# Row-half products issued in pairs, and each attention head's output product moved ahead of a later head's scores

## The chip, the cores and the metric

One core of a Trainium2 chip runs the whole kernel. The metric is device time in microseconds of one execution; the median of the runs shown is compared. Engines are named as in the profile: PE (TensorE, with PEld for its weight loads), DVE (VectorE), ACT (ScalarE), POOL (GpSimd) and SP (SyncE, which issues the weight DMAs).

## What is computed

One encoder layer for 512 prompt tokens and 32 sample tokens (544 columns in all), in float32:

```
h = RMSNorm(x);  c = h @ w_in            # columns: RWKV-7 | q, k, v | gates A, B
A = RWKV-7 time mixing(c)                # per head matrix state, chunks of 64
s = q_n . k_n * 64**-0.5, n = 0, 1       # differential attention, 4 heads, 2 maps
o = (softmax(s_0) - lam * softmax(s_1)) @ v     # block-causal for the prompt
mix = sig(gA) * (A @ w_out_a) + sig(gB) * (RMSNorm(o) @ w_out_b)
x = x + RMSNorm(mix @ w_o);  x = x + RMSNorm(SwiGLU(RMSNorm(x)))
```

Outputs are the new x, the keys, the values and the RWKV states.

## The kernel before

Every large product ("dense") is made of float32 split in two parts, w_hi/w_lo and h_hi/h_lo, with three matmuls for each. POOL splits the weights, 128 columns at a time. The dense products of the whole layer are one long list, and all small work stands between them. The order is written out by hand: `schedule()` makes one list of steps, `SCHEDULE`, and each of the engines runs through the same list and issues its own part of every step. So the list sets the order on PE, and on ACT and DVE too. An engine issues its instructions in that order and waits at each for its semaphores.

Small products write to four PSUM banks, `side0` to `side3`, in a ring: the n-th fill (`FILL`, from `fills()`) uses bank n % 4, `open_bank` makes PE wait until the fill four before it was drained, `full_bank` makes the reader wait until the product is there, `drain` frees the bank and `landed` waits for a drain.

Attention has 16 prompt heads, numbered here 0 to 15: tiles t = 0 to 3 of 128 queries with 4 heads each, with 128(t+1) keys, then 4 heads of the sample tile. One head i consists of these steps:

- `attS` (S): PE makes the two score maps, m = 0 on partitions 0 to 63 and m = 1 on 64 to 127, one bank each (L1124). DVE sets the mask (L1703), takes the maximum (L1705) and scales it (L1706) for each map; ACT makes the exponentials with their sums (L1317), again one map after the other.
- `attC` (C): DVE combines both maps into the weights (L1717 to L1721), in one of two buffers `probs`.
- `attP` (P): PE transposes the weights (L1081, `side<-ident,early`, t+1 of them), ACT copies them to `pT` (L1327).
- `attO` (O): PE multiplies `pT` by v (L1150); it waits until the copy has drained its bank. ACT copies the result to `otok` (L1337) and takes its squares with their sum (L1338).

Between the steps stand pieces of the gate products gB and gA: `piece()` takes as many as `turns` says, 24 for these 16 heads. A piece, D below, is a quarter of a block of 128 columns, 12 matmuls of 272 columns; at the end of a block ACT makes a tanh of it (L1586) and issues its store. The loop for head i puts S two heads ahead:

```python
rows = [piece() + [("attP", *th)], piece()]
...attC(i + 1), attS(i + 2) at the end of the second row
rows += [piece() + [("attO", *th)] + ...]
```

Products that contract over 64 rows ("row halves": their operands stand on partitions 0 to 63 or on 64 to 127) are besides S: `rwA` (L1174: decay, f = "w", rows 0 to 63; and learning rate, f = "a", rows 64 to 127; two column halves each), four times; and in the RWKV part, for each tile t and each half g of the heads, `sk` (L911, f = "k", 256 columns) and `sb1` (L911, f = "r", 128 columns), with p for the row half. ACT's copies of step `tok` (L1421 to L1424) drain the four banks that `sk` then takes, and DVE drains `sk` (L1817) and `sb1` (L1809). An fp32 product stands in the profile as two MATMULs.

Of the kernel before, what the change touches and what calls it, by code (L numbers as in the profile page):

```python
# [9 lines left out]
ACT = mybir.ActivationFunctionType  # L10
# [9 lines left out]
HALF = TOK // 2  # L20
J = TOK + 1
# [11 lines left out]
BH, BD_, BV = 4, 64, 128  # L33
# [11 lines left out]
SAMPLE = NT - 1  # L45
# [156 lines left out]
def schedule():  # L202
# [7 lines left out]
    def spread(n, places):  # L210

        return [(i + 1) * n // places - i * n // places for i in range(places)]
# [31 lines left out]

    pieces = [dense(k, i, p, 4) for k in ("gB", "gA") for i in range(8) for p in range(4)]
    heads = [(t, h) for t in range(NT) for h in range(BH)]
    turns = [1] + spread(24, 3 * BH * SAMPLE) + [2, 1, 1, 1, 1, 0, 1, 1, 1, 1, 1, 1]

    def piece():
        n = turns.pop(0)  # L250
        out, pieces[:n] = pieces[:n], []
        return out
# [3 lines left out]
    for i, th in enumerate(heads):  # L256
        rows = [piece() + [("attP", *th)], piece()]
        if i + 1 < len(heads):
            rows[-1] += [("attC", *heads[i + 1])]
        if i + 2 < len(heads):  # L260
            rows[-1] += [("attS", *heads[i + 2])]
        rows += [piece() + [("attO", *th)] + ([("vtok", th[0] + 1)] if th[0] < SAMPLE and th[1] == 1 else [])]
        if th[0] < SAMPLE:
            s += sum(rows, [])
        else:
            sample += rows
# [55 lines left out]
def fills(step):  # L322

    k = step[0]
    if k == "params":
        return ["pv"]
    if k in ("normB", "zC"):
        return ["n0", "n1"]
    if k == "cache":
        return ["ck"]  # L330
    if k in ("ktok", "vtok"):
        return [k[0]]
    if k == "attS":
        return ["s0", "s1"]
    if k == "attP":
        return ["pt"]
    if k in ("ofin", "attO"):
        return ["o"]
    if k == "shiftout":
        return ["s"]  # L340
    if k == "knorm":
        return ["q0", "q1"]
    if k == "rwA":
        return ["w0", "w1", "a0", "a1"]
    if k == "rw2":
        return ["b0", "b1"]
    if k == "init":
        return ["s"]
    if k == "w":
        return {"tok": ["t0", "t1"], "sb0": ["b0", "b1"], "sb1": ["r0", "r1"], "sk": ["k0", "k1"], "xi": [], "ya": [],  # L350
                "gv": ["gv"], "wu": ["wu"], "e": ["e0", "e1"] if step[2] < SAMPLE else ["e0"], "chain0": ["c"],
                "chain1": ["c"], "q": ["q"], "yb": ["y"]}[step[1]]
    if k in ("wm", "wd", "wt"):
        return [k[1]]
    if k == "final":
        return ["f"]
    if k in ("ymean", "yvar"):
        return ["m"]
    if k == "yfin":
        return ["g"]  # L360
    if k == "ztok":
        return ["z0", "z1"]
    if k == "zw":
        return ["z"]
    return []
# [32 lines left out]
def encoder_kernel(nc, i_, o_):  # L398
# [40 lines left out]
    dtmp = sb("dtmp", [P, J], at=phase2)  # L439
# [24 lines left out]
    vtok = sb("vtok", [P, NT, BW], at=region)  # L464
# [28 lines left out]
    ossq = sb("ossq", [P, NT * BH], at=phase2)  # L493
# [8 lines left out]
    otok = sb("otok", [P, NT, BW], at=inner)  # L502
# [54 lines left out]
    def open_bank(pe, step, f):  # L557

        n = FILL[(step, f)]
        if n >= 4:  # L560
            pe.wait_ge(drained[n % 4], n // 4)
        return side[n % 4]
# [10 lines left out]
    def landed(eng, step, f):  # L573

        n = FILL[(step, f)]
        eng.wait_ge(drained[n % 4], n // 4 + 1)
# [267 lines left out]
    def wkv_pe(pe, step, transposes, close):  # L844

        t, g = step[2], step[3]
        n, j0 = TILES[t][1], first(t)
# [56 lines left out]
        elif st in ("sb1", "sk"):  # L904
            f, blk, us = ("r", CR, slice(1, 2)) if st == "sb1" else ("k", CK, slice(0, 2))
            m = n * (us.stop - us.start)
            for p in range(2):
                b = open_bank(pe, step, f"{f}{p}")
                lo, hi = 64 * p, 64 * p + 64
                for c in range(2):  # L910
                    ins = pe.matmul(b[0:n, c * m:(c + 1) * m].rearrange("p (u i) -> p u i", i=n),  # L911
                                    C[lo:hi, blk + 2 * g + c, 1 + j0:1 + j0 + n], AR[lo:hi, 2 * g + c, us, j0:j0 + n],
                                    start=True, stop=True)
                close(ins, step, f"{f}{p}")
        elif st == "gv":
            b = open_bank(pe, step, "gv")
            landed(pe, ("w", "tok", t, g), "t1")
# [75 lines left out]
    def _(pe):  # L993
# [91 lines left out]
        for step in SCHEDULE:  # L1085
# [81 lines left out]
            elif k == "rwA":  # L1167
                c = step[1]
                if c == 0:
                    pe.wait_ge(s_["lora_a"], 1)  # L1170
                for f, lo in (("w", 0), ("a", 64)):
                    for i, (a, b_) in enumerate(((0, HALF), (HALF, J))):
                        b = open_bank(pe, step, f"{f}{i}")
                        close(pe.matmul(b[:, 0:b_ - a], wa2[lo:lo + 64, c * P:(c + 1) * P],  # L1174
                                        C[lo:lo + 64, CWA, 1 + a:1 + b_], start=True, stop=True), step, f"{f}{i}")
# [65 lines left out]
    def _(act):  # L1241
# [11 lines left out]
        def drain(ins, step, f):  # L1253

            ins.then_inc(drain_sem(step, f), 1)
# [10 lines left out]
        for step in SCHEDULE:  # L1266
# [65 lines left out]
            elif k == "attO":  # L1332
# [1 line left out]
                _, t, h = step  # L1334
                n, idx = TILES[t][1], t * BH + h
                b = full_bank(act, step, "o")
                A(f_act(otok[0:n, t, h * BV:(h + 1) * BV], b[0:n, 0:BV], ACT.Copy))  # L1337
                drain(f_act(b[0:n, 0:BV], b[0:n, 0:BV], ACT.Square, accum_out=ossq[0:n, idx:idx + 1]), step, "o")  # L1338
            elif k == "oscale":
                n, a, b_ = ((P, 0, SAMPLE * BH), (DEC, SAMPLE * BH, NT * BH))[step[1]]  # L1340
                landed(act, ("attO", SAMPLE if step[1] else SAMPLE - 1, BH - 1), "o")
# [729 lines left out]
```

## Time and profile before

| | |
|---|---|
| median of 3 runs | 1038.54 us (1035.91 to 1040.54) |
| the profiled execution | 1040.89 us, its span 1039.1 us |
| PE busy | 993.6 us, 96% of the span |
| DVE, ACT, POOL busy | 451.2, 284.0, 557.1 us |
| granted clock of PE, mean | 0.996 |
| POOL waiting for PE | 366.2 us |

Busy time of PE counts overlapping matmuls once. A row of the timeline merges instructions of a kind that overlap: its start, the length from the first start to the last end, and behind the names the shapes and the count. "idle before" stands in square brackets.

### The profile page before, as it was taken

How to read it: one execution, taken by the hardware profiler on the slowest of the kernel's cores; microseconds unless marked ns; L12 is line 12 of the kernel's file. 1: busy time of each engine (PE TensorE's matmuls, PEld its weight loads, DVE VectorE, ACT ScalarE, POOL GpSimd, SP SyncE). 2: the span in 40 equal slices, each digit the busy share in tenths (PEclk: the TensorE clock that was granted, in tenths of full speed). 3: DMA queues.
4: the chain of work that ended last, by engine and by line, in shares of the span. 5: the costliest groups of instructions: out<-in, count | busy, mean ns of one | idle time of the engine just before them, and what ended most of it. 6: DMA issues, size and time to landing. Idle time of an engine off the chain costs nothing.

```text
span 1039.1 us, 22129 instructions
## 1 busy us (share of the span) xinstructions
PE 993.6 (96%) x8886; PEld 939.6 (90%) x8886; DVE 451.2 (43%) x878; ACT 284.0 (27%) x810; POOL 557.1 (54%) x608
## 2 busy tenths in 40 slices
PE   5999999999999999999989998999999999999997
PEld 5999999987878888888878898999999999999996
DVE  5466478277643555655355354333333333200003
ACT  5223444255554132332211353001101000011101
POOL 6667899633445224143257713655655655656571
PEclk9999999999999999999999999999999999999999
DMA  7332332432223101050115611223223223232332
GB/s 245 86 86 79 82 82 65 133 103 73 66 76 87 33 33 33 33 204 22 47 47 160 177 34 62 81 83 99 81 81 101 81 81 101 74 95 74 94 92 87
DMA packets 138111, 89.63 MB, mean 86 GB/s; under 512 B 5386, under 2 KB 130032, under 8 KB 138032
## 3 DMA queue, kind: packets, MB, share of 16 engines
q1 hardware_dynamic: 129508, 73.11, 24.6%
q10 hardware_dynamic: 8524, 15.42, 4.3%
q8 instruction: 56, 0.92, 0.4%
q14 instruction: 23, 0.19, 0.1%
HBM read 79.32 MB, written 9.19 MB: 85 GB/s over the span
## 4 chain that ended last, share of the span: by engine, by line
PE 82%; DVE 6%; POOL 4%; DMA 3%; ACT 3%; issue 1%; ACTq 0%; DVEq 0%; SPq 0%; POOLq 0%
PE dense L1005 66%; PE side L1081 3%; DMA w_raw<-in_w_o 2%; POOL w_lo L738 1%; PE side L1124 1%; PE side L1150 1%; PE side L957 1%; POOL S L738 1%; PE side L931 1%; PE side L921 1%; PE side L1201 1%; DMA xs<-in_x_prompt 1%; PE side L911 1%; PE side L871 1%; PE side L987 1%
## 5 line engine op out<-in xcount | busy, mean ns | idle before, releaser
L733 POOL TENSOR_SCALAR w_hi<-w_raw 128x256 fp32r<-128x256 f32 (+1 forms) x256 | 160.3, 646 | 374.7 <-PE dense L1005 366.2
L738 POOL TENSOR_TENSOR w_lo<-w_raw,w_hi 128x256 fp32r<-128x256 f32 (+1 forms) x256 | 320.8, 1276 | 9.8
L1005 PE MATMUL dense<-h_hi,w_hi 128*128 128x272 f32 (+2 forms) x1392 | 302.7, 295 | 4.4 <-DVE h_lo L1640 2.5
L1005 PE MATMUL dense<-h_hi,w_lo 128*128 128x272 f32 (+2 forms) x1392 | 293.8, 289 | 0.0
L1005 PE MATMUL dense<-h_lo,w_hi 128*128 128x272 f32 (+2 forms) x1392 | 293.1, 288 | 0.0
L1005 PEld LDWEIGHTS dense<-h_hi,w_hi 128*128 128x128 f32 x1392 | 220.9, 189 | 15.0 <-issue 7.0
L1005 PEld LDWEIGHTS dense<-h_lo,w_hi 128*128 128x128 f32 x1392 | 221.4, 189 | 0.0
L1005 PEld LDWEIGHTS dense<-h_hi,w_lo 128*128 128x128 f32 x1392 | 220.2, 189 | 0.0
L1005 PE MATMUL dense<-S,w_hi 128*128 128x272 f32 (+2 forms) x648 | 109.2, 289 | 0.1
L1005 PEld LDWEIGHTS dense<-S,w_hi 128*128 128x128 f32 x648 | 92.2, 188 | 0.5 <-issue 0.4
L1005 PE MATMUL dense<-S,w_lo 128*128 128x272 f32 (+2 forms) x324 | 68.2, 288 | 0.0
L2001 DVE SCALAR_TENSOR_TENSOR S<-z,S 128x544 f32 (+1 forms) x22 | 53.7, 2440 | 22.4 <-ACT S L1539 22.4
L1995 DVE TENSOR_TENSOR z<-z,dense 128x544 f32<-128x544 f32 (+2 forms) x23 | 15.9, 696 | 97.1 <-PE dense L1005 97.1
L1936 DVE TENSOR_TENSOR z<-side,gain 128x512 f32<-128x512 f32 x7 | 4.8, 692 | 114.6 <-ACT h_hi L1502 114.6
L1005 PEld LDWEIGHTS dense<-S,w_lo 128*128 128x128 f32 x324 | 51.1, 188 | 0.0
L1539 ACT ACTIVATE S<-z 128x544 f32 (+1 forms) x22 | 14.5, 659 | 132.3 <-DVE z L1995 132.3
L1005 PE MATMUL dense<-S 128*128 128x288 f32 (+1 forms) x336 | 45.3, 291 | 1.7 <-POOL S L738 1.7
L1005 PEld LDWEIGHTS dense<-S 128*128 128x128 f32 x336 | 42.8, 188 | 2.5 <-issue 2.2
L1990 DVE SCALAR_TENSOR_TENSOR z<-z,dense 128x544 f32<-128x544 f32 (+2 forms) x23 | 15.9, 697 | 59.0 <-ACT z L1532 55.1
L1532 ACT ACTIVATE z<-dense 128x544 f32<-128x544 f32 x21 | 13.1, 626 | 97.5 <-PE dense L1005 97.5
L816 POOL TENSOR_TENSOR AR<-AR 128x256 f32<-128x256 f32 (+1 forms) x10 | 6.5, 650 | 46.1 <-DVE AR L1889 46.1
L1317 ACT ACTIVATE early<-side,amax 128x128 f32<-128x128 f32 (+4 forms) x40 | 20.0, 499 | 34.8 <-DVE amax L1706 31.8
(269 smaller groups left out, 1392.6 us busy)
## 6 DMA issues: line engine op xcount, KB each, us to landing
w_raw<-in_w_ffn_in SPq DMA_DIRECT2D x44, 512.0 KB, 3.8
w_raw<-in_w_in SPq DMA_DIRECT2D x43, 512.0 KB, 3.9
w_raw<-in_w_ffn_out SPq DMA_DIRECT2D x16, 448.0 KB, 3.7
gates<-gst ACTq DMA_DIRECT2D x16, 272.0 KB, 2.1
w_raw<-in_w_o SPq DMA_DIRECT2D x8, 512.0 KB, 4.3
w_raw<-in_w_ffn_out SPq DMA_DIRECT2D x8, 512.0 KB, 3.8
w_raw<-in_w_out_a SPq DMA_DIRECT2D x5, 512.0 KB, 3.4
mb<-gates ACTq DMA_DIRECT2D x1, 2176.0 KB, 9.9
```

The lines of the kernel that those rows point to most:

```text
L733: ins = nc.gpsimd.tensor_scalar(hi[:, q], w_raw[:, slot, q], 1.0, 0.0, ALU.mult, ALU.add)
L738: ins = nc.gpsimd.tensor_tensor(lo[:, q], w_raw[:, slot, q], hi[:, q].bitcast(F32), ALU.subtract)
L871: ins = pe.matmul(b[32 * q:32 * q + 32, 0:64], xt[:, g, q, :], mce[:, g, q, :], start=True, stop=True)
L911: ins = pe.matmul(b[0:n, c * m:(c + 1) * m].rearrange("p (u i) -> p u i", i=n), C[lo:hi, blk + 2 * g + c, 1 + j0:1 + j0 + n], AR[lo:hi, 2 ...
L1005: ins = pe.matmul(acc[:, bk, 0:tn], w, r[:, t0:t0 + tn], start=first and n == 0, stop=final and n == 2)
L1081: ins = pe.transpose(b[0:m, c0:c0 + n], src, ident[0:n, 0:n])
L1317: drain(f_act(probs[0:n, pb, m, 0:keys], b[0:n, 0:keys], ACT.Exp, bias=amax[0:n, 2 * pb + m:2 * pb + m + 1], scale=SCALE, accum_out=asum[0 ...
L1532: f_act(f_t.rearrange("p (a b) -> p a b", a=2), pa[:, :, 0:HALF], ACT.Tanh, scale=0.5).then_inc(s_["f_tanh"], 1)
L1539: f_act(dst, f_s.unsqueeze(1), ACT.Copy, scale=0.5).then_inc(s_["f_hi"], 1)
L1990: ins = vec.scalar_tensor_tensor(out=fs, in0=ft, scalar=1.0, in1=ga_, op0=ALU.add, op1=ALU.mult)
L1995: ins = vec.tensor_tensor(fs, fs, gb_, ALU.mult)
L2001: vec.scalar_tensor_tensor(out=lo, in0=f_s.unsqueeze(1), scalar=0.5, in1=hi.bitcast(F32), op0=ALU.mult, op1=ALU.subtract).then_inc(s_["f_l ...
```

## The change

1. The order within a head. P(i), C(i+1), then O(i), and S(i+2) last. Before: P(i), C(i+1), S(i+2), O(i). `turns` now gives a head 0, 1 and i % 2 pieces: none ahead of P, one between P and O, and for an odd i one between O and S. Before it alternated 0, 1 over the three places, so that a pair of heads had 0, 1, 0 and 1, 0, 1. The sum is 24 in both. For the sample heads the same loop gives four rows a head in place of three, and these are woven with the steps of the RWKV inverse.
2. `rwA` and `sb1`/`sk` issue their products in turns of low and high row half, having opened both banks; the order of `FILL` for `rwA` follows.
3. In `attO`, ACT drains the bank with the copy, and takes the squares from `otok` in SBUF, into `dtmp`, no longer from the bank.

```diff
--- before.py
+++ after.py
@@ -244,7 +244,7 @@
 
     pieces = [dense(k, i, p, 4) for k in ("gB", "gA") for i in range(8) for p in range(4)]
     heads = [(t, h) for t in range(NT) for h in range(BH)]
-    turns = [1] + spread(24, 3 * BH * SAMPLE) + [2, 1, 1, 1, 1, 0, 1, 1, 1, 1, 1, 1]
+    turns = [1] + [n for i in range(BH * SAMPLE) for n in (0, 1, i % 2)] + [2, 1, 1, 1, 1, 0, 1, 1, 1, 1, 1, 1]
 
     def piece():
         n = turns.pop(0)
@@ -257,9 +257,8 @@
         rows = [piece() + [("attP", *th)], piece()]
         if i + 1 < len(heads):
             rows[-1] += [("attC", *heads[i + 1])]
-        if i + 2 < len(heads):
-            rows[-1] += [("attS", *heads[i + 2])]
-        rows += [piece() + [("attO", *th)] + ([("vtok", th[0] + 1)] if th[0] < SAMPLE and th[1] == 1 else [])]
+        rows += [[("attO", *th)] + ([("vtok", th[0] + 1)] if th[0] < SAMPLE and th[1] == 1 else [])]
+        rows += [piece() + ([("attS", *heads[i + 2])] if i + 2 < len(heads) else [])]
         if th[0] < SAMPLE:
             s += sum(rows, [])
         else:
@@ -341,7 +340,7 @@
     if k == "knorm":
         return ["q0", "q1"]
     if k == "rwA":
-        return ["w0", "w1", "a0", "a1"]
+        return ["w0", "a0", "w1", "a1"]
     if k == "rw2":
         return ["b0", "b1"]
     if k == "init":
@@ -904,14 +903,15 @@
         elif st in ("sb1", "sk"):
             f, blk, us = ("r", CR, slice(1, 2)) if st == "sb1" else ("k", CK, slice(0, 2))
             m = n * (us.stop - us.start)
-            for p in range(2):
-                b = open_bank(pe, step, f"{f}{p}")
-                lo, hi = 64 * p, 64 * p + 64
-                for c in range(2):
-                    ins = pe.matmul(b[0:n, c * m:(c + 1) * m].rearrange("p (u i) -> p u i", i=n),
+            b = [open_bank(pe, step, f"{f}{p}") for p in range(2)]
+            for c in range(2):
+                for p in range(2):
+                    lo, hi = 64 * p, 64 * p + 64
+                    ins = pe.matmul(b[p][0:n, c * m:(c + 1) * m].rearrange("p (u i) -> p u i", i=n),
                                     C[lo:hi, blk + 2 * g + c, 1 + j0:1 + j0 + n], AR[lo:hi, 2 * g + c, us, j0:j0 + n],
                                     start=True, stop=True)
-                close(ins, step, f"{f}{p}")
+                    if c == 1:
+                        close(ins, step, f"{f}{p}")
         elif st == "gv":
             b = open_bank(pe, step, "gv")
             landed(pe, ("w", "tok", t, g), "t1")
@@ -1168,8 +1168,8 @@
                 c = step[1]
                 if c == 0:
                     pe.wait_ge(s_["lora_a"], 1)
-                for f, lo in (("w", 0), ("a", 64)):
-                    for i, (a, b_) in enumerate(((0, HALF), (HALF, J))):
+                for i, (a, b_) in enumerate(((0, HALF), (HALF, J))):
+                    for f, lo in (("w", 0), ("a", 64)):
                         b = open_bank(pe, step, f"{f}{i}")
                         close(pe.matmul(b[:, 0:b_ - a], wa2[lo:lo + 64, c * P:(c + 1) * P],
                                         C[lo:lo + 64, CWA, 1 + a:1 + b_], start=True, stop=True), step, f"{f}{i}")
@@ -1334,8 +1334,9 @@
                 _, t, h = step
                 n, idx = TILES[t][1], t * BH + h
                 b = full_bank(act, step, "o")
-                A(f_act(otok[0:n, t, h * BV:(h + 1) * BV], b[0:n, 0:BV], ACT.Copy))
-                drain(f_act(b[0:n, 0:BV], b[0:n, 0:BV], ACT.Square, accum_out=ossq[0:n, idx:idx + 1]), step, "o")
+                drain(f_act(otok[0:n, t, h * BV:(h + 1) * BV], b[0:n, 0:BV], ACT.Copy), step, "o")
+                landed(act, step, "o")
+                A(f_act(dtmp[0:n, 0:BV], otok[0:n, t, h * BV:(h + 1) * BV], ACT.Square, accum_out=ossq[0:n, idx:idx + 1]))
             elif k == "oscale":
                 n, a, b_ = ((P, 0, SAMPLE * BH), (DEC, SAMPLE * BH, NT * BH))[step[1]]
                 landed(act, ("attO", SAMPLE if step[1] else SAMPLE - 1, BH - 1), "o")
```

PE in tile 3, around the scores of head 14 (`qkv 128x512`; `vtok,pT` is an O, `ident,early` a P). Before:

```order
L1124 MATMUL side<-qkv 128x512 x2
L1150 MATMUL side<-vtok,pT 128x128 x4
L1005 MATMUL dense<-h_hi,w_hi 128x272 x2
L1005 MATMUL dense<-h_lo,w_hi 128x272 x2
L1005 MATMUL dense<-h_hi,w_lo 128x272 x2
L1005 MATMUL dense<-h_hi,w_hi 128x272 x2
L1005 MATMUL dense<-h_lo,w_hi 128x272 x2
L1005 MATMUL dense<-h_hi,w_lo 128x272 x2
L1081 MATMUL side<-ident,early 128x128 x4
L1124 MATMUL side<-qkv 128x512 x2
```

After:

```order
L1150 MATMUL side<-vtok,pT 128x128 x4
L1124 MATMUL side<-qkv 128x512 x2
L1081 MATMUL side<-ident,early 128x128 x4
L1005 MATMUL dense<-h_hi,w_hi 128x272 x2
L1005 MATMUL dense<-h_lo,w_hi 128x272 x2
L1005 MATMUL dense<-h_hi,w_lo 128x272 x2
L1005 MATMUL dense<-h_hi,w_hi 128x272 x2
L1005 MATMUL dense<-h_lo,w_hi 128x272 x2
L1005 MATMUL dense<-h_hi,w_lo 128x272 x2
L1150 MATMUL side<-vtok,pT 128x128 x4
```

Before, the rows are S(14), O(12), a piece, P(13), S(15), and O(13) comes only after one more piece. After, they are O(12), S(14), P(13), a piece, O(13).

ACT over the same heads (`early,asum` are the two exponentials of a head, `pT` the copy of a P, `otok` that of an O). Before:

```order
L1327 ACTIVATE pT<-side 128x512
L1586 ACTIVATE gst<-dense,pvh 128x544
L1589 DMA gates<-gst 128x544
L1317 ACTIVATE early,asum<-side,amax 128x512 x2
L1337 ACTIVATE otok<-side 128x128
L1338 ACTIVATE side,ossq<-side 128x128
L1327 ACTIVATE pT<-side 128x512
L1317 ACTIVATE early,asum<-side,amax 128x512 x2
```

After:

```order
L1327 ACTIVATE pT<-side 128x512
L1587 ACTIVATE gst<-dense,pvh 128x544
L1590 DMA gates<-gst 128x544
L1337 ACTIVATE otok<-side 128x128
L1339 ACTIVATE dtmp,ossq<-otok 128x128
L1317 ACTIVATE early,asum<-side,amax 128x512 x2
L1327 ACTIVATE pT<-side 128x512
L1337 ACTIVATE otok<-side 128x128
```

Before, the rows begin with `pT` of head 12 and the tanh; the exponentials are those of head 14, then `otok` of 12, `pT` of 13 and the exponentials of 15. After, they begin with the same two, and `otok` of 12 has moved ahead of the exponentials of 14, with `pT` and `otok` of 13 behind them. In both orders `pT` of head i+1 stands behind the exponentials of head i+2.

## Rows read from the trace of the kernel before

**Rows 1.** The page, parts 1 and 2: TensorE's busy time and granted clock.

```profile
PE 993.6 (96%) x8886; PEld 939.6 (90%) x8886; DVE 451.2 (43%) x878; ACT 284.0 (27%) x810; POOL 557.1 (54%) x608
...
PEclk9999999999999999999999999999999999999999
```

**Rows 2.** Timeline, tile 3: start us, length us, engine, line, operation, tiles, count.

```profile
257.08 0.60 PE L1081 MATMUL side<-ident,early 128*128 128x128 f32 x4
...
259.04 0.59 ACT L1327 ACTIVATE pT<-side 128x512 f32<-128x512 f32 x1
...
259.11 1.13 PE L1124 MATMUL side<-qkv 64*128 64x512 f32 x4
...
260.17 1.16 PE L1150 MATMUL side<-vtok,pT 128*128 128x128 f32 x8
...
260.46 0.11 DVE L1703 MEMSET side<- 64x64 f32 x1
...
261.08 0.49 PE L1005 MATMUL dense<-h_hi,w_hi 128*128 128x272 f32 x2
...
262.67 0.60 PE L1081 MATMUL side<-ident,early 128*128 128x128 f32 x4
262.69 0.69 ACT L1317 ACTIVATE early<-side,amax 128x512 f32<-128x512 f32 x1 [0.33 <-DVE amax L1706]
...
263.20 1.45 PE L1124 MATMUL side<-qkv 64*128 64x512 f32 x4
...
264.85 0.75 DVE L1721 SCALAR_TENSOR_TENSOR early<-early,arec 128x512 f32<-128x512 f32 x1
```

**Rows 3.** Timeline, tile 0, second head.

```profile
202.27 0.49 PE L1124 MATMUL side<-qkv 64*128 64x128 f32 x4
...
202.69 0.52 PE L1005 MATMUL dense<-h_hi,w_hi 128*128 128x272 f32 x2
202.91 0.11 DVE L1703 MEMSET side<- 64x64 f32 x1 [1.48 <-PE side L1124]
...
204.33 0.37 ACT L1317 ACTIVATE early<-side,amax 128x128 f32<-128x128 f32 x1 [0.24 <-DVE amax L1706]
```

**Rows 4.** Timeline, tile 2: a copy of weights and the output products behind it.

```profile
239.69 0.48 ACT L1327 ACTIVATE pT<-side 128x384 f32<-128x384 f32 x1
...
240.28 0.91 PE L1150 MATMUL side<-vtok,pT 128*128 128x128 f32 x6
```

**Rows 5.** ScalarE by form, 202 to 269.5 us: xcount | busy us, mean ns.

```profile
L1327 ACT ACTIVATE pT<-side 128x128 f32<-128x128 f32 x4 | 1.1, 273 | 1.4 <-DVE vtok L1690 1.4
```

**Rows 6.** TensorE by form, the same stretch: score products.

```profile
L1124 PE MATMUL side<-qkv 64*128 64x512 f32 x16 | 5.8, 641 | 0.0
L1124 PE MATMUL side<-qkv 64*128 64x384 f32 x16 | 5.0, 535 | 0.0
L1124 PE MATMUL side<-qkv 64*128 64x256 f32 x16 | 4.0, 428 | 0.0
...
L1124 PE MATMUL side<-qkv 64*128 64x128 f32 x12 | 2.0, 323 | 0.0
```

**Rows 7.** Timeline of TensorE: a full-row fp32 product, then the other row-half products.

```profile
57.56 1.08 PE L1165 MATMUL side<-AR,cst 128*128 128x272 f32 x4
...
116.67 1.20 PE L1174 MATMUL side<-C,wa 64*128 64x272 f32 x8
...
327.26 3.00 PE L911 MATMUL side<-AR,C 64*128 64x256 f32 x16 [0.42 <-ACT tok L1421]
...
368.03 2.45 PE L911 MATMUL side<-AR,C 64*128 64x256 f32 x16
...
372.12 1.26 PE L911 MATMUL side<-AR,C 64*128 64x128 f32 x16
```

**Rows 8.** Timeline of ScalarE ahead of the `sk` products of tile 1.

```profile
368.92 0.39 ACT L1424 ACTIVATE ag<-side 128x256 f32<-128x256 f32 x1
```

**Rows 9.** 530.5 to 533.3 us: length, busy PE, PEld, DVE, ACT, POOL; granted clock; DMA.

```profile
530.50:533.30 2.80, 0.77 (x9) 0.56 (x7) 1.21 (x4) 1.03 (x5) 2.63 (x4) 1.00 0.00 0
```


## The prediction

> **What bounds the kernel now.** I read the page first: PE is busy 993.6 of 1039.1 us at a granted clock of 9 and more tenths in every slice [rows 1]. PE is the bound nearly everywhere, so each microsecond that its stream gains or loses between two dense products is one of the kernel. The question is therefore how long PE stands or runs half filled in the stretches that the change touches: the attention of heads 1 to 15 (about 202 to 269 us), `rwA`, and `sk`/`sb1`.
>
> Next the timeline of tile 3, where the attention steps are longest [rows 2]. The reader is to follow one head through three engines. S(14) starts on PE at 259.11 and the next step 1.06 us later. DVE starts on its maxima at 260.46, ACT ends the exponential of its second map at 262.69 + 0.69 = 263.38. Only then can ACT copy the transposed weights of head 13, since that copy stands behind these exponentials in its list. The same is seen one head earlier: P(12) is made at 257.08 and ready by 257.7, but its copy starts at 259.04. PE doesn't feel it now, because O(12) comes only at 260.17, after a piece and S(14), and O(13) after P(13), S(15) and another piece. PE's present loss in attention is another one: S(15) takes 1.45 us, where S(14) takes 1.13. The second map waits for the bank that the exponential of the head before still reads, so the two halves of the array don't run side by side.
>
> **The change, part by part.**
>
> *The new place of O.* After the change PE's list is S(i+1), P(i), a piece, O(i), then S(i+2). ACT's is exponentials(i+1), copy(i), `otok`(i). O(i) needs copy(i), copy(i) stands behind exponentials(i+1), and these need S(i+1), which PE now issues only one P and one piece ahead. And S(i+2) stands behind O(i) on PE. That is a closed ring, one turn for each head: whatever the chain takes beyond PE's own work between S(i+1) and O(i) is idle time of PE.
>
> The chain, for 512 keys: from the start of S to DVE's start 1.28 us (the products take 1.13 [rows 2], the wait behind them 0.15: in tile 0 S starts at 202.27, takes 0.49, and DVE starts at 202.91 [rows 3]; in tile 3 DVE was late by 0.07 from its earlier work). From there to the end of the second exponential 263.38 - 260.46 = 2.92 [rows 2]. The copy takes 0.59 [rows 2], and O starts 0.10 behind a copy (239.69 + 0.48 to 240.28 [rows 4]). Sum 4.89 us. For 128 keys: 0.64, then 204.33 + 0.37 - 202.91 = 1.79 [rows 3], 0.27 for the copy [rows 5], 0.10: 2.80. Tiles 1 and 2 lie evenly between: 3.50 and 4.20.
>
> PE's work in that time: S 1.06 in tile 3 [rows 2], 0.42 in tile 0 (202.27 to 202.69 [rows 3]); P at 0.11 for each key tile, 0.11 to 0.44 (four and the switch take 262.67 to 263.20 [rows 2]); a piece 1.59 (261.08 to 262.67 [rows 2]). Sums: 2.12, 2.44, 2.77 and 3.09 us for tiles 0 to 3.
>
> The wait of PE before O: 0.68, 1.06, 1.43 and 1.80 us. S(i+1) is in tile 0 for i = 0 to 2, in tiles 1 to 3 for four heads each: 3 x 0.68 + 4 x (1.06 + 1.43 + 1.80) = 19.2 us. For i = 15 the scores ahead are those of the sample, with a short chain but the long copy: 0.7 as an estimate, near tile 0. Together 19.9 us. Whether the second piece of an odd head stands between O and S doesn't matter, since it lies outside of the span that waits. P(i) itself doesn't wait: C ends some 2 us after the exponentials (264.85 + 0.75 against 263.38 [rows 2]), and P(i) is asked for after a copy, an O of 0.9 and an S of 1.06.
>
> That copy(i) waits behind exponentials(i+1) rests on ACT keeping its order. The Trainium skill, "TensorE: Matmul & The Clock Gate", in its table and its part on queue depths, says that ScalarE is strictly first in, first out and that only TensorE reorders, and there only weight loads; the copy at 259.04 agrees.
>
> *What the new order gives back.* When S(i+2) is issued, O(i) has run, so copy(i) and both exponentials(i+1) are done and both banks are free. All scores are then made side by side. The groups of S now take 5.8, 5.0, 4.0 and 2.0 us for 4, 4, 4 and 3 heads [rows 6]; side by side a head takes 1.13 [rows 2], 0.49 [rows 3], and 0.92 and 0.70 between. 1.28 + 1.32 + 1.20 + 0.53 = 4.3 us come back.
>
> *Pairs in `rwA`, `sk`, `sb1`.* Two full-row products (four MATMULs of 272 columns) take 1.08 us; the four row-half products of `rwA` (eight MATMULs) take 1.20 [rows 7]. So the two halves already run side by side although the list has them one after the other: zero. The same for `sb1`: sixteen MATMULs of 128 columns in 1.26 [rows 7]. `sk` isn't full, 3.00 and 2.45 us for sixteen of 256 [rows 7]. But it is held by its banks: its last pair waits for ACT's last copy of `tok`, which ends at 369.31 [rows 8], and ends 1.2 us later, at 370.48, which is what four passes take. Opening both banks first can't make that earlier: zero, at worst a few tenths, since the first bank of a pair starts later.
>
> The Trainium skill, "TensorEngine Tiling (Array Packing)", Theoretical Speedup, gives up to 2x for products that contract over 64 rows or less. For `rwA` and `sb1` this case's trace shows that factor as taken already.
>
> *The squares.* One ACT instruction reads SBUF in place of PSUM and the bank is free some 0.4 us sooner; nobody waits for that bank now, as the next O has its turn much later. Zero.
>
> *The sample heads.* Same ring, but RWKV steps and pieces stand between, and there is more than a piece between P and O in most. I take zero, between -1.5 and +1.5 us (a wait of about 1 us in either direction around the weave).
>
> Sum: +19.9 - 4.3 = +15.6 us on 1040.9 for the profiled execution (its span of 1039.1 and 1.8 around it), 1056.5. It stands 2.35 above the median of the runs, 1038.54, so **1054 us** for the median.
>
> **Rivals.**
>
> *The pairs win, and O doesn't wait.* If the copy were ready when the piece ends, the 4.3 us of the scores would stay, and with full pairs in `sk` (eight rounds at 0.213 and 0.2 of filling, 1.9 against 3.00 + 3 x 2.45 [rows 7]) 2.7 more: 1038.5 - 7.0 = 1031.5. It ends on the other side. The point from which it decides: a mean wait before O below 4.3 / 16 = 0.27 us. Against it stands the copy at 259.04, already 1.4 us late with a piece and S still to come [rows 2]. The skill's page on array packing is the rule that would lead here.
>
> *The two cancel.* The chain would have to be 1 us shorter a head than read, for instance since DVE starts map 0 before map 1 is ready and ACT's work between is shorter. Then 16 x 0.25 = 4 us are lost, 4.3 come back: 1038.
>
> *PE's clock falls.* PE would stand about 1.4 us in each 4 to 6 us over 75 us. Were the clock granted at 1.2 instead of 2.4 GHz there, some 50 us of its work would take twice as long: 1100. Against it: from 530.5 to 533.3 us PE was busy 0.77 of 2.80 us and the granted clock stayed 1.00 [rows 9].
>
> *More waits.* ACT's tanh at a block's end and the store behind it come into the ring for six heads, at about 1 us each, or the sample loses 1.5: 1060.
>
> **How the numbers follow.** Forecast (the ring waits, between half a microsecond less and a few tenths more a head) 0.80, with 1060 in it; pairs win 0.08; cancel 0.10; clock 0.02. The forecast's own range: each wait 0.4 shorter, -6.4, gives 1047.5; the tanh in the ring, +6, 1060. The range 1047 to 1061 leaves out the other cases, 0.20 in all. A measurement of this kernel tells 0.5% (5 us) from no change: faster 0.08, within 0.10, slower 0.82.
>
> **What would show it.** In the changed profile: idle time of PE ahead of L1150, in nearly each head, of 0.7 us in tile 0 to 1.8 in tile 3; O starting 0.1 us behind L1328, the copy, and that copy right behind the second exponential; S at 1.13 us for 512 keys in all heads; `rwA` still 1.20 and `sb1` 1.26, `sk` near 2.4. The stretch from S(14) to S(16) grows by about 3 us. It is wrong if copies start before the exponentials of the next head end, if PE has no idle time at O, or if `rwA` shrinks.

## The result

The changed kernel takes 1052.29 us, the median of 4 runs (1051.14 to 1053.97), against 1038.94 for 4 runs of the kernel before on the same chip (1035.91 to 1040.54). The ratio is 1.0134, with a 95% interval of 1.0117 to 1.0152: slower by 13.4 us. The profiled execution took 1053.97.

The page of the changed kernel, its span, the busy times and the granted clock; they answer to [rows 1]:

```profile
span 1052.1 us, 22157 instructions
...
PE 991.5 (94%) x8886; PEld 936.0 (89%) x8886; DVE 449.3 (43%) x878; ACT 285.6 (27%) x810; POOL 555.8 (53%) x608
...
PEclk9999999999999999999989999999999999999999
```

PE's busy time is 2.1 us less than before, and the span 13.0 us more. So nothing was added to PE's work; PE waits.

The timeline around the scores of head 12 (start us, length us, engine, line, operation, tiles; idle before in brackets), which answers to [rows 2]:

```profile
258.82 1.13 PE L1124 MATMUL side<-qkv 64*128 64x512 f32 x4
...
259.88 0.55 PE L1081 MATMUL side<-ident,early 128*128 128x128 f32 x3
260.12 0.11 DVE L1704 MEMSET side<- 64x64 f32 x1 [0.62 <-PE side L1124]
...
262.35 0.69 ACT L1317 ACTIVATE early<-side,amax 128x512 f32<-128x512 f32 x1 [0.30 <-DVE amax L1707]
...
263.02 0.48 ACT L1327 ACTIVATE pT<-side 128x384 f32<-128x384 f32 x1
...
263.65 0.91 PE L1150 MATMUL side<-vtok,pT 128*128 128x128 f32 x6 [1.71 <-ACT pT L1327]
...
265.99 1.13 PE L1124 MATMUL side<-qkv 64*128 64x512 f32 x4
```

This is the ring. S(12) runs at 258.82, DVE begins its maxima at 260.12, the second exponential of head 12 starts at 262.35, and the copy of head 11's weights, made by PE at 259.88 to 260.43, comes only behind it, at 263.02. PE has stood for 1.71 us when O(11) starts, 0.15 us behind the copy's end (263.50). S(13) follows a piece after O(11), at 265.99.

PE's groups from 202 to 291 us (xcount | busy us, mean ns | idle before): the products O, and the four widths of scores, which answer to [rows 6]:

```profile
L1150 PE MATMUL side<-vtok,pT 128*128 128x128 f32 x80 | 12.7, 290 | 16.2 <-ACT pT L1327 12.3 <-issue 3.9
...
L1124 PE MATMUL side<-qkv 64*128 64x512 f32 x16 | 5.2, 737 | 0.0
L1124 PE MATMUL side<-qkv 64*128 64x384 f32 x16 | 3.7, 535 | 0.0
L1124 PE MATMUL side<-qkv 64*128 64x256 f32 x16 | 2.8, 428 | 0.0
...
L1124 PE MATMUL side<-qkv 64*128 64x128 f32 x12 | 1.5, 322 | 0.0
```

16.2 us of idle stand ahead of the O products; before the change the same products, to 269 us, had 0.1. What `<-issue` names (3.9 us, three O's) are waits for a copy too: the one at 270.88 us starts 0.10 us behind the end of its copy. The other side shows too: the scores take 5.2 + 3.7 + 2.8 + 1.5 = 13.2 us where they took 16.8.

One such wait for each tile of the scores that stand ahead of it, tiles 0 to 3 in order:

```profile
209.50 0.46 PE L1150 MATMUL side<-vtok,pT 128*128 128x128 f32 x2 [0.53 <-ACT pT L1327]
...
228.78 0.68 PE L1150 MATMUL side<-vtok,pT 128*128 128x128 f32 x4 [0.98 <-ACT pT L1327]
...
239.60 0.68 PE L1150 MATMUL side<-vtok,pT 128*128 128x128 f32 x4 [1.34 <-ACT pT L1327]
...
285.50 1.13 PE L1150 MATMUL side<-vtok,pT 128*128 128x128 f32 x8 [1.70 <-ACT pT L1327]
```

Two points that both programs pass give the sum of the stretch: the scores of head 1, at 202.27 in [rows 3], and the second transpose of `xp`, which in the kernel before is

```profile
282.33 0.33 PE L1081 MATMUL side<-ident,xp 128*128 128x128 f32 x1 [0.86 <-DVE xp L1803]
```

and in the changed kernel both are

```profile
201.98 0.49 PE L1124 MATMUL side<-qkv 64*128 64x128 f32 x4
...
299.43 0.33 PE L1081 MATMUL side<-ident,xp 128*128 128x128 f32 x1 [0.86 <-DVE xp L1804]
```

282.33 - 202.27 = 80.06 us before, 299.43 - 201.98 = 97.45 after: **+17.4 us in the attention of the prompt**, and -4.1 us from there to the end of the program (17.1 at that transpose, 13.0 in the span).

The 4.1 us have two parts. The sample heads stand between that transpose and the first transposes of `otok`, which start, before and after, at

```profile
309.52 0.66 PE L1081 MATMUL side<-ident,otok 128*128 128x128 f32 x4
```

```profile
324.90 0.66 PE L1081 MATMUL side<-ident,otok 128*128 128x128 f32 x4
```

The difference is 15.4 us here and was 17.1 at the transpose of `xp`: the sample heads give 1.7 us back. In this stretch PE waits 0.41, 0.32 and 0.60 us in the kernel before (at 292.99, 297.89 and 308.94) and only 0.35 in the changed one (at 322.58). The other 2.4 us come later. The prediction has the attention of the prompt in its sum and the sample heads at zero; the 2.4 us are not in it.

### The profile page after: what moved, and what is told of

It is laid out like the page before. It is cut to its first block, busy times and chain, and to the rows that moved or that the text cites. A ratio compares the mean times of both kernels' runs of the same rounds, so it can differ in the third digit from the quotient of the medians.

```text
span 1052.1 us, 22157 instructions
## 1 busy us (share of the span) xinstructions
PE 991.5 (94%) x8886; PEld 936.0 (89%) x8886; DVE 449.3 (43%) x878; ACT 285.6 (27%) x810; POOL 555.8 (53%) x608
## 4 chain that ended last, share of the span: by engine, by line
PE 81%; DVE 6%; POOL 4%; ACT 3%; DMA 2%; issue 2%; ACTq 0%; DVEq 0%; SPq 0%; POOLq 0%
PE dense L1005 65%; PE side L1081 3%; DMA w_raw<-in_w_o 1%; PE side L1150 1%; POOL w_lo L737 1%; PE side L1124 1%; DVE amax L1706 1%; PE side L910 1%; PE side L957 1%; POOL S L737 1%; PE side L931 1%; PE side L921 1%; PE side L1201 1%; DMA xs<-in_x_prompt 1%; ACT early L1317 1%
## 5 line engine op out<-in xcount | busy, mean ns | idle before, releaser
L1533 ACT ACTIVATE z<-dense 128x544 f32<-128x544 f32 x21 | 13.2, 626 | 97.4 <-PE dense L1005 97.4
L1150 PE MATMUL side<-vtok,pT 128*128 128x128 f32 (+1 forms) x88 | 14.3, 289 | 16.2 <-ACT pT L1327 12.3
```

The costliest lines, as they stand in the source:

```text
L1150: ins = pe.matmul(b[0:n, 0:BV], pT[0:kn, pb, i * n:(i + 1) * n], v, start=i == 0, stop=i == len(kts) - 1)
L1533: f_act(f_t.rearrange("p (a b) -> p a b", a=2), pa[:, :, 0:HALF], ACT.Tanh, scale=0.5).then_inc(s_["f_tanh"], 1)
```

## The experiments

All are compared with the kernel before in the same chip session.

| kernel | median us | ratio, 95% interval |
|---|---|---|
| changed | 1052.29 | 1.0134 (1.0117 to 1.0152) |
| old order, pairs and squares | 1038.23 | 0.9987 (0.9972 to 1.0001) |
| new order alone | 1056.59 | 1.0167 (1.0146 to 1.0187) |
| changed, ACT's copy one step earlier | 1040.73 | 1.0009 (0.9997 to 1.0021) |
| changed, all pieces between P and O | 1043.60 | 1.0033 (1.0015 to 1.0051) |
| before, squares | 1040.44 | 1.0018 (0.9999 to 1.0036) |
| before, all pairs | 1037.14 | 0.9982 (0.9970 to 0.9994) |
| changed, squares undone | 1053.39 | 1.0138 (1.0117 to 1.0159) |
| before, all pairs, pieces ahead of S | 1038.56 | 0.9995 (0.9981 to 1.0008) |
| before, pairs in `sk`, `sb1` | 1036.71 | 0.9978 (0.9964 to 0.9992) |
| before, pairs in `rwA` | 1040.42 | 0.9994 (0.9978 to 1.0010) |
| before, 20 idle waits on PE | 1035.98 | 0.9968 (0.9952 to 0.9984) |
| new order alone, 20 idle waits | 1054.12 | 1.0132 (1.0110 to 1.0154) |

### Which part of the change costs the time

**The order undone, the rest kept.**

```diff
-    turns = [1] + [n for i in range(BH * SAMPLE) for n in (0, 1, i % 2)] + [2, 1, ...]
+    turns = [1] + spread(24, 3 * BH * SAMPLE) + [2, 1, ...]
...
-        rows += [[("attO", *th)] + ...]
-        rows += [piece() + ([("attS", *heads[i + 2])] if i + 2 < len(heads) else [])]
+        if i + 2 < len(heads):
+            rows[-1] += [("attS", *heads[i + 2])]
+        rows += [piece() + [("attO", *th)] + ...]
```

> The changed kernel with the old order of steps and pieces; the pairs in rwA, sk and sb1 and the squares from SBUF stay. If the new order is the whole loss (my theory), the time is that of before within 0.3%, 1038 to 1042 us. If the pairs gain what the array could give, 1032 to 1036. If the delay of the sk products that the changed profile hints at is real (the dense product behind sk and sb1 starts later against the start of the tile, about 1.2 us in all four tiles), 1040 us and the same delay is in this trace.

1038.23 us: the loss is gone. The delay of `sk` that the expectation speaks of is in this trace too, a wait of 1.20 us ahead of the first `sk` (at 329.76); the experiments on the pairs come back to it.

**The order alone**, the two other parts left as before (the first diff turned round).

> The kernel before with the new order of steps and pieces alone. My theory: O waits for the copy as in the changed kernel (0.7 us in tile 0 to 1.9 in tile 3), 1050 to 1053 us. If the pairs or the squares have a part in the loss, 1048 or less. All 15 score groups take their paired length, 1.13 us for 512 keys, since both banks are free.

1056.59 us, which is 3 to 4 us above what was expected and above the changed kernel. The new order costs 17 us by itself. Its groups and the same two points:

```profile
L1149 PE MATMUL side<-vtok,pT 128*128 128x128 f32 x80 | 12.7, 289 | 17.0 <-ACT pT L1326 13.0 <-issue 3.9
...
L1123 PE MATMUL side<-qkv 64*128 64x512 f32 x16 | 4.5, 641 | 0.0
...
202.74 0.49 PE L1123 MATMUL side<-qkv 64*128 64x128 f32 x4
...
299.51 0.33 PE L1080 MATMUL side<-ident,xp 128*128 128x128 f32 x1 [0.86 <-DVE xp L1802]
```

The scores take 4.5 + 3.7 + 2.8 + 1.5 = 12.5 us, 4.3 less than before. The stretch takes 299.51 - 202.74 = 96.77, +16.7 us, much as in the changed kernel. At the transposes of `otok` (325.67) the two kernels agree: from the scores of head 1 on, both have lost 15.7 us. The 3 to 4 us lie behind that, and the experiments under "What gives 3 us back" look for them.

### Is it the ring over ACT's list?

**ACT's copy one step earlier.** Only ACT's list changes: where the exponentials of head i+2 stand directly ahead of the copy of head i+1, the two change places. PE and DVE keep the new order.

```diff
-        for step in SCHEDULE:
+        act_steps = list(SCHEDULE)
+        for n in range(len(act_steps) - 1):
+            if act_steps[n][0] == "attS" and act_steps[n + 1][0] == "attP":
+                act_steps[n], act_steps[n + 1] = act_steps[n + 1], act_steps[n]
+        for step in act_steps:
```

> The changed kernel with one thing moved on ACT alone: where the exponentials of head i+2 and the copy of head i+1 follow each other, the copy comes first. PE's and DVE's orders stay. My theory (the copy is late because it stands behind the exponentials): the waits of PE ahead of O vanish in tiles 0 to 3, what remains is the chain of DVE and ACT of about 4.9 us a head in tile 3; 1038 to 1044 us. Rival (O is late because it stands only one piece behind P, whatever ACT does before): waits of the same size, 1050 to 1054.

1040.73 us. Nearly all of the loss goes with two entries of ACT's list changing places, so the copy's place behind the exponentials is the wait, and not, say, the products themselves or their banks. The groups, of the same stretch:

```profile
L1150 PE MATMUL side<-vtok,pT 128*128 128x128 f32 x80 | 11.6, 276 | 0.0
L1081 PE MATMUL side<-ident,early 128*128 128x128 f32 x40 | 7.8, 293 | 7.4 <-DVE early L1726 7.4
```

No idle is left ahead of O. What is left, 7.4 us, stands ahead of P and is waiting for DVE's last step of C. The timeline of heads 12 and 13 shows why:

```profile
257.65 0.60 ACT L1331 ACTIVATE pT<-side 128x512 f32<-128x512 f32 x1 [2.34 <-PE side L1081]
...
258.26 0.69 ACT L1321 ACTIVATE early<-side,amax 128x512 f32<-128x512 f32 x1
...
261.86 1.09 DVE L1726 SCALAR_TENSOR_TENSOR early<-early,arec 128x512 f32<-128x512 f32 x1
...
263.01 0.66 PE L1081 MATMUL side<-ident,early 128*128 128x128 f32 x4 [1.69 <-DVE early L1726]
```

The copy at 257.65 no longer waits for exponentials; these start behind it, at 258.26, and so C(13) ends late (261.86 + 1.09) and P(13) is late by 1.69 us. That is the longest of these waits, since the last step of C takes 1.09 us here and 0.75 at the other heads with 512 keys (the last section shows why). The ring is shorter, but it is still a ring: the copy of one head, the exponentials, C and P of the next.

**The same pieces, all between P and O.**

```diff
-    ... for n in (0, 1, i % 2)] ...
+    ... for n in (0, 1 + i % 2, 0)] ...
```

> The changed kernel with the second piece of an odd head between P and O in place of between O and S, so (0, 2, 0) for odd and (0, 1, 0) for even heads. My theory (the wait is a chain from S, and only work between S and O covers it): odd heads lose up to 1.5 us of their wait each, even heads none, 9 us in all, 1041 to 1046 us. Rival (PE is short of work as a whole in attention and waits for the same chain wherever the pieces stand): no gain, 1050 to 1054.

1043.60 us. The prediction said that it doesn't matter for the wait whether the second piece of an odd head stands between O and S, since it lies outside of the span that waits. The reverse is what this uses: put inside the span, a piece of 1.6 us covers the wait of that head. The group of O:

```profile
L1150 PE MATMUL side<-vtok,pT 128*128 128x128 f32 x80 | 12.4, 286 | 8.2 <-ACT pT L1327 4.4 <-issue 3.7
```

Half of the 16.2 us are left, nearly all at the heads that have one piece.

### What gives 3 us back

**The squares alone, all pairs alone, and the change without the squares.** The diffs are the parts 3 and 2 of the change, and part 3 taken back.

> The kernel before with one part of the change, the sum of squares that reads the copy in SBUF where it read the PSUM bank. The changed kernel was 3 to 4 us faster than the kernel with the new order alone, and the kernel with the old order and the other parts 1.4 us faster than before; something beside the order gives this back. Theory A, the squares do: 1036 to 1038, and the copy of the last state (ACT, written to dtmp) no longer waits 3.6 us for its store, so the identity products of C behind it don't wait 1.2 us. Theory B, the pairs in rwA, sb1 and sk do: 1038.5 to 1040, with that wait of 3.6 us as before.

> The kernel before with another part of the change, the row halves paired in rwA, sb1 and sk. Theory A (the squares give the 1.4 to 4 us back): 1038.5 to 1040.5, since gv starts later by what the first bank of each pair now waits. Theory B (the pairs do): 1036 to 1038.

> The changed kernel with the squares put back to the PSUM bank; new order and pairs stay. Theory A (the squares give back): 1055 to 1058, as the new order alone. Theory B (the pairs do): 1051.5 to 1053, as the changed kernel.

1040.44, 1037.14 and 1053.39 us. Theory B: the squares give nothing (1.0018, with 1 in the interval), the pairs 1.9 us in the old order and, from 1.0167 to 1.0138, 3 in the new. The intervals of the last two touch, but the changed kernel has the same pairs and came out at 1.0134.

**The pairs taken apart.**

> The kernel before with the pairs in sb1 and sk alone. Pairs everywhere gave 1.9 us. Theory A (these pairs give it, by the work or through what stands behind it at the end of a block): 1036.5 to 1038, and the store of the first last state lands 1.8 us after its issue. Theory B (rwA's give it): 1039 to 1040, and that store takes 3.6 us as before.

> The kernel before with the pairs in rwA alone. Theory A (sb1 and sk give the 1.9 us): as before, 1038.5 to 1040, rwA at 1.20 us for each step and the store of the first last state at 3.6 us. Theory B (rwA's give it): 1036.5 to 1038.

1036.71 and 1040.42 us: `sk` and `sb1` give it, `rwA` nothing (by the medians; the two intervals overlap, and only the first leaves out 1). But their own products don't explain it. In the changed kernel `sk` of tile 0, `sb1` behind it, and an `rwA` step, against [rows 7]:

```profile
343.45 2.32 PE L910 MATMUL side<-AR,C 64*128 64x256 f32 x16 [1.20 <-ACT ag L1425]
...
347.39 1.16 PE L910 MATMUL side<-AR,C 64*128 64x128 f32 x16
...
116.42 1.19 PE L1174 MATMUL side<-C,wa 64*128 64x272 f32 x8
```

`sk` falls from 3.00 to 2.32 us and `sb1` from 1.26 to 1.16, while the wait ahead of `sk` grows from 0.42 to 1.20, since both banks must be open before the first product. In tile 0 that is even. Over all tiles it is a small loss. With the pairs in `sk` and `sb1` alone, their products take 9.1 + 4.7 us where they took 10.3 + 5.1. But PE waits 1.7 us ahead of `sk` where it waited 0.4, and 2.3 us ahead of the products behind `sb1` (L921, which wait for DVE's `rb`) where it waited 1.3. From the scores of head 1 to the ten identity products of `C` near 497 us it takes 498.04 - 202.47 = 295.57 us, against 496.97 - 202.27 = 294.70 before: 0.9 us more. The gain comes elsewhere, 150 us after the first `sk`. Here is the kernel before, where ACT stores the first finished state (a start behind `ACTq` is a DMA issue):

```profile
495.54 0.39 ACTq L1247 DMA_DIRECT2D out_wkv_prompt<-dtmp  x1
...
499.06 0.27 ACT L1458 ACTIVATE dtmp<-side 64x128 f32<-64x128 f32 x1 [3.56 <-DMA out_wkv_prompt<-dtmp]
...
499.69 0.51 PE L1081 MATMUL side<-ident,C 128*32 128x128 f32 x3 [1.25 <-ACT dtmp L1459]
```

The second copy of a state reuses the buffer and waits 3.56 us for the store, and PE's identity products of `C` wait 1.25 us behind it. In the kernels with the pairs in `sk` that store lands 1.77 us after ACT went idle, and PE doesn't wait. The DMA view from 496.3 to 498.3 us tells what is in the way. First come the GB/s in 40 slices of 0.05 us, then the queues (packets, MB, share of 16 engines' time):

```profile
GB/s 328 0 10 102 179 241 195 195 190 93 26 0 0 0 0 0 0 0 0 0 0 0 0 0 0 0 0 0 0 5 5 10 5 10 10 5 15 5 10 0
...
q10 hardware_dynamic: 272, 0.07, 16.9%
q8 instruction: 1, 0.02, 4.6%
```

Beside the 272 packets of the store there is one of another queue, marked instruction: 16 KB of the program's code. It takes 4.6% of 16 engines' 2.0 us, 1.5 us on one of them. A packet's bytes are counted where it starts, so the 328 is the 16 KB packet. Most of the store's packets have started after 0.55 us; then none starts for 0.9 us, and the last ones follow one by one from 497.75 on, as the 16 KB come to their end. The kernels before, with the order alone, with the squares alone and with `rwA`'s pairs have such a packet among the store's; those with `sk`'s pairs have none. A second store of the same size agrees. That of the sample's first state (issued at 533.15 us in the kernel before) has such a packet beside it in all 14 kernels, with or without pairs, and ACT waits 3.2 to 3.8 us behind it in all of them (in two the trace names PE, and not the store, as what ended the wait).

The pages give the number of executed instructions: 22129 before, 22149 with all pairs, and 22129 with those of `rwA` alone. Opening both banks of `sk` and `sb1` first makes 20 more waits, so later code is fetched at another moment. That can be tried without any pair.

**Twenty waits that wait for nothing.**

```diff
             m = n * (us.stop - us.start)
+            pe.wait_ge(s_["lora_a"], 1)
             for p in range(2):
```

> The kernel before with nothing changed but one more wait of PE, on a semaphore that has long been reached, ahead of each sk and sb1 step, 20 in all, as many instructions as the pairs in sk and sb1 add to PE's list. Computation, order and pairs are as before. In the traces so far the store of the first last state took 3.0 to 3.6 us without those pairs, with a 16 KB instruction packet among its own in the DMA queues, and 1.8 us with them, with no such packet. Theory (the pairs give their 2 us by their instructions, which move the fetch of code out of that store): no instruction packet beside the store, 1.8 us, no wait of PE for dtmp ahead of C's identity products, the sk products at 10.3 us as before, 1035.5 to 1038. Rival (the pairs themselves do it): the store at 3.0 to 3.6 us, 1039 to 1040.5.

1035.98 us, the lowest median here: 0.9968 (0.9952 to 0.9984). Its profiled execution has a span of 1035.9 us and 22149 instructions. The store and what waits for it, and the DMA view of the same two microseconds:

```profile
495.93 0.38 ACTq L1248 DMA_DIRECT2D out_wkv_prompt<-dtmp  x1
...
497.67 0.27 ACT L1459 ACTIVATE dtmp<-side 64x128 f32<-64x128 f32 x1 [1.77 <-DMA out_wkv_prompt<-dtmp]
```

```profile
q10 hardware_dynamic: 272, 0.07, 15.8%
```

No instruction packet, 1.77 us instead of 3.56, and PE goes on. The packet that the kernel before has at 496.3 runs at 492.9 here, ahead of the store. The 0.9 us that the pairs cost are not lost (497.37 - 202.61 = 294.76). Twenty more instructions give as much as the pairs or more.

**The same in the new order.**

> The kernel with the new order alone (no pairs, squares as before; 1056.6) and the same 20 waits of PE, one ahead of each sk and sb1 step. Theory (the changed kernel is some 3 us faster than the order alone because the pairs' instructions move the fetch of code): 1052 to 1054, the store of the first last state at 1.8 us, PE's waits ahead of O as in the changed kernel. Rival (in the new order the pairs' own work gives it): 1055.5 to 1058.

1054.12 us, a tenth above the theory's range: ratio 1.0132 against 1.0167 for the order alone (the intervals just touch) and 1.0134 for the changed kernel. The store lands in 1.77 us, without an instruction packet. The 3 us by which the change is better than its order alone are no merit of its pairs.

### Paired scores without the ring

**The kernel before with the pairs, and both pieces of a head ahead of its scores**: P(i), one or two pieces, S(i+2), O(i).

```diff
-    turns = [1] + spread(24, 3 * BH * SAMPLE) + [2, 1, ...]
+    turns = [1] + [n for i in range(BH * SAMPLE) for n in (0, 1 + i % 2, 0)] + [2, 1, ...]
```

> The kernel before with the pairs in rwA, sb1 and sk, and with both pieces of a head ahead of the scores: P(i), one or two pieces, S(i+2), O(i). The scores then start when the exponentials of the head before have read their banks, so the two row halves run side by side, and O(i) keeps a step between itself and its copy. Theory (what the new order gives back, 4.3 us, is the paired scores and can be had without its ring): S at about 1.1 us for 512 keys, no wait of PE ahead of O, 1032 to 1036. Rival (the maxima start up to a piece later, so C(i+1) is late for P(i+1)): waits of PE ahead of the transposes of C, 1037 to 1041.

1038.56 us, no better than the 1037.14 of the same pairs with the old places. The theory was wrong in size, and the rival in its cause:

```profile
L1082 PE MATMUL side<-ident,early 128*128 128x128 f32 x40 | 7.3, 280 | 2.9 <-ACT early L1318 2.7
L1125 PE MATMUL side<-qkv 64*128 64x512 f32 x16 | 5.0, 641 | 0.0
```

The scores shrink only in part, for 512 keys from 5.8 to 5.0 us. And 2.7 us of waits appear ahead of P, at four heads, not for C, as the rival had it, but for the first exponential of the next head. The four are those behind `vtok`, whose product takes one more place in the ring of the four banks. With it P(i+1) comes four fills after the first map of S(i+2), so it must wait until ACT has read that map. Put a piece later, these scores are read later. What was gained is given back there.

## Why the prediction was right

1054.0 was forecast, 1052.29 came, within 1047 to 1061. By its steps:

- *The ring.* Right in mechanism. The copy stands right behind the second exponential of the next head, O behind the copy by 0.10 to 0.15 us (in the changed kernel the copy is L1327, not L1328, as the prediction wrote), and moving two entries of ACT's list takes the wait away. The Trainium skill, "TensorE: Matmul & The Clock Gate", Architectural detail, says that ACT's queue is strictly first in, first out; that experiment agrees.
- *The size of the waits.* 0.68, 1.06, 1.43 and 1.80 us were forecast for tiles 0 to 3; the brackets above read 0.53, 0.98, 1.34 and 1.70. Ahead of a wait the last dense product also runs out (0.27 us or so, where the next product would have started 0.12 after it), some 0.15 us a wait that the brackets leave out. With it, 0.68, 1.13, 1.49 and 1.85. The sum was to be 19.9; it is 16.2 + 15 x 0.15 = 18.4 in the changed kernel and 17.0 + 2.2 = 19.2 with the order alone. The last head waits 0.23 and not 0.7, and head 0 not at all, where the sum had 0.68 for it.
- *What comes back in the scores.* 4.3 was forecast, and 16.8 - 12.5 = 4.3 came with the order alone. In the changed kernel's trace it was 3.6: one pair of scores for 512 keys fell into a moment of lower clock (the mean of a product is 737 ns and not 641).
- *"P(i) itself doesn't wait."* Wrong in one head of tile 0: P stands 0.89 us there, in both kernels with the new order, for DVE's C, three steps of which took twice their usual time or more (the last section). The prediction had worked the slack out for tile 3 only.
- *The stretch.* 18.4 - 3.6 + 0.9 = 15.7 of the 17.4 us are these rows. The lower clock (last section) took 0.4 + 0.5 + 0.5 + 0.3 = 1.7 us of PE, of which 0.7 is already in the scores: 1.0 more. 0.7 us is not assigned. The slower work also filled part of one wait: O at 277.60 waits 0.84 us, and 1.57 with the order alone.
- *The sample heads: zero.* They gave 1.7 us back, 1.0 with the order alone, from 17.1 to 15.4 us between the two transposes. That is beyond the 1.5 that the prediction allowed them.
- *`rwA`, `sb1`: zero.* Right: 1.19 and 1.16 us where they took 1.20 and 1.26. *`sk` near 2.4*: 2.32.
- *Pairs are worth nothing, at worst a few tenths.* This is the term that was most wrong: -2 to -3 us. The pairs' own work costs 0.9 us, since the waits grow more than the products shrink. The gain comes with 20 added waits, which moved a fetch of code out of a store; that explains about half of it. No row of the trace of before that the prediction looked at could show it; the DMA view at a store does.
- *The rivals.* "The pairs win" and "the two cancel" needed a mean wait below 0.27 us or a shorter chain; it was over 1. With full pairs `sk` took 2.32 us and not the 1.9 of that rival. "PE's clock falls" came true for some 4 us, not for 75, and cost 1 us or less: the stretch is 0.7 us longer than with the order alone, whose clock stayed full there. "ACT's tanh comes into the ring" didn't show: the waits of the heads with a tanh don't stand out.

The forecast of 1054 came so near in part by luck, since misses cancel: the stretch was 1.8 us worse than the sum of 15.6, the sample heads gave 1.7 back, and what lies behind them 2.4. For the order alone the first two leave 15.7 us, next to the 15.6 of the sum; its median, 1056.59 us, is still 2.5 above the forecast, which had taken off 2.35 us as the distance of the median from the profiled execution.

What stays open: of the 3.2 us that the 20 waits gave in the profiled executions, the store and PE's wait behind it are about 1.5. The rest comes in small steps after 530 us, at waits for the weights that POOL prepares, and I haven't traced it to transfers. Single executions differ by as much there: that of the squares alone has a span of 1035.3 us, with the packet beside its store, though its median shows no gain.

## What to carry to other kernels

Before an operation is moved ahead on one engine, write down the lists of all engines it depends on: a consumer pulled forward doesn't run sooner than its producer's place in another engine's list, and if the next item is put behind it, the chain becomes a ring whose full length is paid each turn. Ask then whether the producer can be moved with it; here that was two entries of ACT's list and 12 us. And when a part of a change that should be worth nothing gains or loses 2 us, add the same number of idle instructions to the old kernel before believing in the part.

## What the runs showed of the hardware

**Code fetches get in the way of small stores.** A store of 64 KB that lands in 1.77 us took 3.56 us when one 16 KB instruction packet ran at the same time, and 20 instructions more or less on PE decided whether they met. It is the tail that is held up: 0.9 us without a start, then the last packets. The Trainium skill has both halves: "Runtime: NRT & Kernel Launch", Terms, says that instruction memory is refilled in 16 KiB blocks, and "DMA: Bandwidth & Descriptors", Queues, rings and completion order, that each DMA engine takes whole packets from its queues in turn. The trace agrees: one packet of 16 KB, 1.5 us, and the store was late by 1.8. The 0.9 us without a start fit an engine that finishes the large packet first.

**DVE's steps take longer beside POOL's `w_lo`.** The head of tile 0 whose P waited, in the changed kernel: an ordinary last step of C, then the two slow ones with the POOL instructions that ran beside them, and P:

```profile
210.04 0.35 DVE L1722 SCALAR_TENSOR_TENSOR early<-early,arec 128x128 f32<-128x128 f32 x1
...
213.66 2.77 POOL L737 TENSOR_TENSOR w_lo<-w_raw,w_hi 128x256 fp32r<-128x256 f32 x4
...
215.12 0.71 DVE L1721 TENSOR_SCALAR early<-early,arec 128x128 f32<-128x128 f32 x1
...
215.87 0.71 DVE L1722 SCALAR_TENSOR_TENSOR early<-early,arec 128x128 f32<-128x128 f32 x1
...
216.64 0.33 PE L1081 MATMUL side<-ident,early 128*128 128x128 f32 x1 [0.89 <-DVE early L1722]
```

The last step takes 0.35 us without POOL and 0.71 beside POOL's `w_lo`. The step ahead of it (L1721) takes 0.71 instead of 0.29, and the small one ahead of that (L1719) 0.41 instead of 0.16. Together these are 1.0 us, enough for the 0.89 that P waits. The Trainium skill, "SBUF — State Buffer", Two separate sides, says that DVE and GpSimd share a pair of ports as an exclusive lock, which an instruction of DVE with two SBUF inputs needs. The last step, which has two such inputs and is lengthened while POOL runs, agrees, and by 0.36 us, about half of one of the four `w_lo` instructions (2.77 / 4 = 0.69); no run here tests the lock by itself. An engine's schedule that looks free can so depend on where POOL happens to be.

**PE's clock fell after a wait, not in it.** The changed kernel by windows (length; busy PE, PEld, DVE, ACT, POOL; granted clock; DMA):

```profile
270.00:271.00 1.00, 0.12 (x1) 0.15 (x2) 0.51 (x3) 1.00 (x4) 0.92 (x4) 1.00 0.00 0
271.00:272.00 1.00, 1.00 (x10) 0.88 (x10) 0.97 (x1) 0.39 (x1) 1.00 (x2) 1.00 0.00 0
272.00:273.00 1.00, 1.00 (x5) 0.24 (x4) 0.99 (x1) 0.68 (x3) 1.00 (x2) 0.60 0.72 270
274.00:275.00 1.00, 1.00 (x6) 1.00 (x6) 0.92 (x3) 0.00 (x0) 0.37 (x1) 0.50 0.00 0
275.00:276.00 1.00, 1.00 (x8) 1.00 (x7) 0.86 (x3) 0.78 (x2) 0.00 (x0) 0.69 0.47 102
```

At 270 us PE was busy 0.12 of 1.00 us at the full clock, and at 271 fully busy, still at the full clock. From 273 to 275 it was fully busy at 0.50, that is 1.2 GHz, and before 276 the clock began to come back. The kernel with the order alone has waits of the same size, and a mean clock of 1.00 from 200 to 300 us. This isn't a property of the program. The kernel with the order alone and 20 idle waits gives PE the same list as the order alone up to the first `sk`, near 343 us, and its clock fell where that of the changed kernel did:

```profile
274.00:275.00 1.00, 1.00 (x6) 1.00 (x5) 0.85 (x4) 0.15 (x1) 0.43 (x1) 0.50 0.00 0
```

The kernel with the old order, pairs and squares, whose longest wait of PE shortly before was 0.86 us, also ran at 0.50 from 284 to 286 us. So whether a microsecond or two is lost to the clock differs from one execution to the next, and a single profiled execution can't give the price of a change to that accuracy.
